# New order of the last attention pair's steps in a one-core decoder kernel, with its output halves, weight halves and row sums

## The reference

```python
for blk in range(S // Q_BLOCK):                       # Q_BLOCK = 128, 8 blocks
    s = einsum(q[:, :, q0:q1], k[:, :, :q1]) * scale  # 16 heads of 64
    s = s + c[:, :, q0:q1, None] - c[:, :, None, :q1] # forget gates, cumulated
    p = softmax(where(mask, s, -inf))
    outs.append(einsum(p, v[:, :, :q1]))
o = concatenate(outs)...reshape(B, S, D_MODEL)
h = h + o @ w_o
h = h + swiglu(rmsnorm(h, norm_ffn[layer]), w_ffn_in[layer], w_ffn_out[layer])
```

## Time and profile before

| | us |
|---|---|
| median of 3 runs | 2259.54 (2257.51 to 2260.15) |
| the profiled execution, its own time | 2259.69 |
| its span, first to last instruction | 2257.9 |
| TensorE busy | 2211.3 (98%) |
| DVE, ACT, POOL busy | 1684.8, 1182.4, 364.0 |
| mean granted TensorE clock | 0.997 |

### The profile page before, as it was taken

How to read it: one execution, slowest core, us unless ns; L and a number is a source line. 1 busy time by engine, 2 the same in 40 slices (tenths; PEclk the granted TensorE clock), 3 DMA queues, 4 the chain that set the end, 5 groups by cost and what they waited for, 6 DMA issues and landing times.

```text
span 2257.9 us, 28937 instructions
## 1 busy us (share of the span) xinstructions
PE 2211.3 (98%) x10409; PEld 1836.0 (81%) x10409; DVE 1684.8 (75%) x2345; ACT 1182.4 (52%) x1871; POOL 364.0 (16%) x353
## 2 busy tenths in 40 slices
PE   8999999999999999999999999989999999999998
PEld 6788877788888888878888888867888888888886
DVE  7667778777778887687766767664768888888866
ACT  5543466355555555256666666653525555555525
POOL 4000000022222222021111111102101222222210
PEclk9999999999999999999999999999999999999999
DMA  5120301366666666331111111122135666666662
GB/s 150 47 59 27 92 4 35 131 131 131 130 131 131 131 131 128 115 113 29 38 29 38 38 38 37 29 93 66 56 112 108 127 130 128 126 132 127 129 170 84
DMA packets 208828, 207.85 MB, mean 92 GB/s; under 512 B 9688, under 2 KB 153280, under 8 KB 208704
## 3 DMA queue, kind: packets, MB, share of 16 engines
q0 software_dynamic: 39168, 75.51, 20.3%
q1 hardware_dynamic: 167808, 126.43, 18.9%
q10 hardware_dynamic: 1728, 4.31, 0.8%
HBM read 122.28 MB, written 83.95 MB: 91 GB/s over the span
## 4 chain that ended last, share of the span: by engine, by line
PE 85%; DVE 8%; ACT 3%; issue 2%; DMA 1%; ACTq 1%; POOL 0%; DVEq 0%
PE ps L1207 36%; PE ps L1039 16%; PE ps L1295 14%; PE ps L1407 7%; PE ps L1452 3%; PE ps L1439 3%; PE ps L1539 2%; PE ps L1419 1%; PE ps L1420 1%; DVE rxl L2223 1%; ACT kh L2068 1%; DVE qs L2949 1%; DMA rinv_dram<-rinv_rows 0%; DVE resid L2243 0%; PE ps L1379 0%
## 5 line engine op out<-in xcount | busy, mean ns | idle before, releaser
L967 POOL DMA_DIRECT2D spill<-c x256 | 224.1, 928 | 727.6 <-DVE c L2613 498.4
L2482 DVE TENSOR_TENSOR ring_l<-raw_ffn,ring_h 128x512 fp32r<-128x512 f32 x320 | 223.1, 699 | 154.3 <-ACT ring_h L1766 152.9
L1766 ACT ACTIVATE ring_h<-raw_ffn 128x512 fp32r<-128x512 f32 x320 | 198.8, 625 | 198.8 <-PE ps L1207 103.9
L1859 ACT ACTIVATE c<-ps 128x512 f32<-128x512 f32 x256 | 150.2, 597 | 13.2
L2104 ACT ACTIVATE probs<-ps,nmax 128x896 f32<-128x896 f32 (+7 forms) x128 | 95.1, 743 | 103.5 <-DVE nmax L3018 101.7
L1407 PE MATMUL ps<-xh,wh_att 128*128 128x512 f32 x368 | 148.8, 404 | 0.0
L1766 ACT ACTIVATE ring_h<-w_sum 128x512 fp32r<-128x512 f32 x112 | 69.6, 625 | 146.6 <-PE ps L1039 38.9
L1407 PE MATMUL ps<-xl,wh_att 128*128 128x512 f32 x368 | 144.1, 392 | 0.0
L1407 PE MATMUL ps<-xh,wl_att 128*128 128x512 f32 x368 | 144.0, 391 | 0.0
L3025 DVE TENSOR_TENSOR ptl<-ps,pth 128x512 fp32r<-128x512 f32 (+1 forms) x160 | 97.1, 635 | 58.2 <-ACT pth L2139 57.1
L2613 DVE TENSOR_TENSOR c<-ps,c 128x512 f32<-128x512 f32 x192 | 123.6, 686 | 4.7 <-PE ps L1295 4.4
(11 more groups left out here) (400 smaller groups left out, 6352.4 us busy)
## 6 DMA issues: line engine op xcount, KB each, us to landing
spill<-c POOLq DMA_DIRECT2D x256, 256.0 KB, 5.9
raw_ffn<-in_w_ffn_in SPq DMA_DIRECT2D x88, 512.0 KB, 5.3
raw_ffn<-in_w_ffn_out SPq DMA_DIRECT2D x44, 512.0 KB, 7.5
resid<-spill SPq DMA_DIRECT2D x24, 512.0 KB, 7.3
raw<-in_w_rec_in SPq DMA_DIRECT2D x16, 512.0 KB, 5.5
spill<-resid POOLq DMA_DIRECT2D x16, 512.0 KB, 2.9
raw_att<-in_w_kvf SPq DMA_DIRECT2D x16, 512.0 KB, 4.0
xin<-in_x SPq DMA_DIRECT2D x4, 1024.0 KB, 9.9
```

The lines of the kernel that those rows point to most:

```text
L967: pool.dma_start(spill[m, :, half * BANK:(half + 1) * BANK], block[:, :], accum_op=ALU.add).then_inc(sem, 16)
L1766: act.activation(F.ring_h[slot][:, :], src, ACT.Copy).then_inc(F.unit_hi, 1)
L1859: act.activation(dst[:, :], y if what == "s5" else w, ACT.Copy).then_inc(out_tapped, 1)
L2482: dve.tensor_tensor(F.ring_l[slot][:, :], src, F.ring_h[slot][:, :].bitcast(F32), ALU.subtract).then_inc(F.unit_lo, 1)
```

## The change

It gives the last pair's units a new order of steps, with the same steps in each unit except for p, of which units now have 2, 5, 1, 6, 3, 4, 4 and 3 where they had 5, 2, 4, 3, 5, 2, 4 and 3. It moves the halves of the output and of the output weights to other steps. R comes ahead of the last unit's T0, and R's transpose waits for the second exponential of that unit too (in every pair). In the last pair ACT issues the row sums' store at V1. DVE adds output tile 0 ahead of the low half of weight 3. For the other pairs the list is unchanged.

```diff
 LAST_UNIT_STEPS = [
-    "T0 T1 X Y p p p T2 V0 V1 T3 S0 S1 p V2 p V3",
-    "O T0 S0 S1 p V0 p",
-    "O T0 T1 S0 p V0 T2 S1 p V1 p V2 p",
-    "O T0 T1 S0 S1 p V0 p V1 p",
-    "O T0 T1 p p V0 T2 p V1 T3 S0 p V2 S1 p V3",
-    "O T0 S0 S1 p V0 p",
-    "O T0 T1 S0 p V0 T2 S1 p V1 p V2 p",
-    "O T0 T1 R p V0 p V1 p",
+    "T0 T1 X Y S0 T2 p T3 V0 V1 p S1 V2 V3",
+    "O p T0 S0 S1 p V0 p p p",
+    "O T0 T1 p V0 T2 V1 S0 S1 V2",
+    "O p p T0 T1 S0 p S1 p V0 p V1 p",
+    "O T0 T1 S0 p T2 V0 T3 V1 p S1 V2 V3 p",
+    "O T0 S0 S1 p p V0 p p",
+    "O T0 T1 S0 p p T2 V0 S1 p p V1 V2",
+    "O p R T0 T1 p p V0 V1",
 ]
...
-HIGH_O_AT = {(-1, "S1"): (0, 1), (-1, "B"): (2,), (0, "Y"): (3,), (0, "T3"): (4,), (1, "V0"): (5,),
-             (2, "V0"): (6,), (3, "S1"): (7,)}
-LOW_O_AT = {(-1, "S1"): (0,), (-1, "B"): (1, 2), (0, "T2"): (3,), (0, "S1"): (4,), (2, "T0"): (5,),
-            (2, "V2"): (6,), (3, "V0"): (7,)}
+HIGH_O_AT = {(-1, "A"): (0, 1), (-1, "B"): (2, 3), (0, "V1"): (4,), (2, "V0"): (5,), (3, "T1"): (6,),
+             (4, "T3"): (7,)}
+LOW_O_AT = {(-1, "S1"): (0,), (-1, "B"): (1,), (0, "S0"): (2,), (0, "V3"): (3, 4), (2, "S1"): (5,),
+            (3, "V1"): (6,), (5, "O"): (7,)}
...
-    OUT_HI_AT = {(-1, "A"): 0, (0, "S1"): 1, (UNITS - 1, "T0"): 2}
-    OUT_LO_AT = {(-1, "S1"): 0, (2, "O"): 1, (UNITS - 1, "T1"): 2}
+    OUT_HI_AT = {(-1, "A"): 0, (0, "Y"): 1, (UNITS - 2, "T2"): 2}
+    OUT_LO_AT = {(-1, "S1"): 0, (1, "S1"): 1, (UNITS - 2, "V2"): 2}
...
                     elif step == "R":
                         acc = claim(rsum_tile(i))
+                        slot, n = s_tile(i, UNITS - 1, 1)
+                        pe.wait_ge(drained[slot], n)
...
-                    if (u, step) == (UNITS - 1, "R"):
+                    if (u, step) == (UNITS - 1, "R" if with_p else "V1"):
                         act.wait_ge(drained[rsum_tile(i)[0]], rsum_tile(i)[1])
...
             for k in range(KT):
+                if k == 0:
+                    dve.wait_ge(reloaded[k], 32)
+                    add_tile(tiles.use("attE", k), k, OUT_ATT + k + 1)
                 if k < KT - 2:
                     if k != 2:
                         split_lo(pieces.use("attE", k + (3 if k < 2 else 2)))
                 else:
                     for n in range(2):
                         first_low(F1, 2 * (k + 2 - KT) + n)
-                dve.wait_ge(reloaded[k], 32)
-                add_tile(tiles.use("attE", k), k, OUT_ATT + k + 1)
+                if k > 0:
+                    dve.wait_ge(reloaded[k], 32)
+                    add_tile(tiles.use("attE", k), k, OUT_ATT + k + 1)
```

## The result

The changed kernel takes 2247.69 us (median of 5 runs, 2247.3 to 2248.19) against 2259.54 (2257.51 to 2261.14): ratio 0.9947, 95% interval 0.9936 to 0.9958. That is 11.85 us less, where 11.0 were forecast (2248.5, range 2245.5 to 2253.5). The profiled execution has a span of 2245.9 us, 12.0 less than before.

What follows compares the result with a forecast made beforehand. TensorE was taken as the bound, losing 14.3 us in the last pair and its tail. Gains of 1.0 + 0.3 + 4.2 + 2.7 + 1.2 + 0.6 + 1.0 = 11.0 us gave 2259.54 - 11.0 = 2248.5 us, range 2245.5 to 2253.5.

Steps and rivals of the forecast that it cites:

- Output halves at the start: Start of the last pair: high halves 0 and 1 made earlier, X waits 0.2 instead of 1.2 us; 1.0 gained.
- Unit 0: Last pair's first unit: V0's wait is spread over T2, V0 and V2; 1.35 of 1.65 us stay, 0.3 gained.
- Units 1 and 2: Last pair: stops before T2.0, p7 and V2.2 go; 4.8 us of stops become 0.6, 4.2 gained.
- Units 3 to 6: Last pair: p steps ahead of each T0 cover the exponentials; 3.2 us of stops become 0.5, 2.7 gained.
- The reload of tile 0: SP's reload of resid, landing about when DVE's early sum 1 wants it: taken as covered, 1.0 us at worst.
- Unit 7 and R: Last unit: stops before V7.0 (0.5 us) and the first wo matmul (0.7) both go; 1.2 gained.
- The added wait in the other seven pairs: R's new wait for the second drain: taken as 0, bound 0.05 us a pair; skill estimate up to 0.8 over eight pairs.
- Tail: Row sums to output: the k = 7 matmuls' 1.2 us stop shrinks; 0.6 gained, 0.7 stays, DMAs 0.5 either way.
- First sum: First output tile's sum ahead of a weight half, so tile 3 no longer starts late: 1.0 us gained, 0.1 perhaps lost.
- The layout: Four queues laid out in order from trace durations: 14.8 us of stops for the old order, trusted to about half a microsecond.

Runs made afterwards that it cites:

- the steps alone: The kernel before with only the new order of steps, R's place and wait, and ACT's store at V1: 2256.19 us, ratio 0.9986.
- the further order: The changed kernel with another order of steps and other places of output and weight halves: 2246.18 us, 0.9939; run again, 2245.64 us.
- the first sum: The kernel before with only the sum of output tile 0 moved ahead of weight half 3: 2258.83 us, ratio 0.9995.
- the output halves alone: The kernel before with only the new places of the output halves: 2256.52 us, ratio 0.9986.
- the order with V behind T: The changed kernel with every V straight behind its T and all p steps at their unit's end: 2269.82 us, ratio 1.0041.

## Why the prediction was right

The sum was 14.3 us of stops less 3.3; in the trace after they are some 2.7 (the four waits and what the pipeline loses at each, and five hesitations under 0.3), and the pair length fell by 11.61. The other 0.24 of the 11.85 is of the size of the 0.31 by which the two profiled executions were apart ahead of the pair.

- *Output halves at the start:* 0.2 was to stay before X, 0.29 did. *Unit 0:* T2, V0 and V2 were to lose 0.7, 0.5 and 0.15, and lose 0.57, 0.42 and 0.23.
- *Units 1 and 2:* 0.2 before p7 and 0.4 before V2.0; measured 0.13 and 0.37. *Units 3 to 6:* 0.1 and 0.4; measured 0.09 and 0.20. The reload of tile 0 is not waited for.
- *Unit 7 and R:* both stops gone, R at 1511.50 (1511.6 forecast), reciprocal to 1512.79 (1512.9). But the parts of this line are not worth the same. With the old units, R and store (everything but the order of steps) the first output matmul does not wait either, and the stop at the first k = 7 matmul is 0.1 us. With R and the store moved and weight half 2 left, in the steps alone, the first output matmul still waits 0.5. So it is weight half 2, made in unit 6, that takes the stop before the first output matmul away, and the new units that take V7.0's (0.37 stays with the old ones); no run shows a gain from R's new place.
- *The added wait in the other seven pairs* was taken as 0: the R transposes of the last five of them are 61.53 to 61.60 us apart, and 61.56 to 61.64 before. From the first to the seventh it is 369.80 us, before 369.87. The Trainium skill's 50 to 100 ns for a sequencer's read of a semaphore ("Advanced Engine Details and Errata", section "Network/Comms") would, if it stood in line once a pair, have made that 0.3 to 0.6 us longer (an estimate), and it is not.
- *Tail, the mis-sized term:* 0.7 was to stay and 0.34 did. The step that was wrong is "the broadcast is issued behind ACT's last o_low (1515.26)": it is issued 0.06 us after o_low starts, at 1514.93, 0.33 earlier. The DMAs themselves took 4.78 us to POOL's start; 4.66 were assumed. In the second trace of the changed kernel they took 4.55, and the stop was 0.1. Over the fourteen traces they took 4.48 to 5.38, so part of how small this stop is belongs to the execution and not to the order.
- *First sum:* 1.0 gained and nothing lost; tile 3 starts as the last k = 7 matmul lets it (1528.37, then 1528.82, two matmuls of 0.23).
- *The layout against the others:* by its own totals of stops (14.8 us before, 3.0 in the changed kernel, 2.0 in the further order) its difference to the pair length of before was within 0.8 us wherever the clock stayed at 1.00 (the further order is the 0.8), and wrong by 1.1 and 6.3 where it fell. The misses of the runs with the first sum (0.3) and the output halves alone (0.4) are no larger than what the wait for the row sums grew: the broadcast took 4.97 and 5.38 us there, where the layout has 4.66.

What the prediction's parts don't say, and the runs do: a part's price hangs on the others. The output halves were given 1.0 for X and bits of other lines; alone they are worth 2.9, and taking them from the changed kernel costs 4.4. The steps alone are worth 3.3, and their loss costs 4.2. The places where a half is made were fitted to the new order, and each without the other brings a stop of its own: 1.6 us before p4 with the halves alone, 1.5 before T2 with the steps alone.

## What to carry to other kernels

When several in-order engines follow one written list, lay the queues out by the durations of the trace before changing the list, and check the layout on the old order first: here that gave 14.8 us of stops for an 80 us stretch where the trace has 14.3. Move list and side work together, since each alone brings new stops. Look for the independent matmuls (p steps) that stand where nothing waits, and put them between the transposes or scores and the step that waits for their results.

## What was not expected of the hardware

The granted TensorE clock can fall in the midst of a busy kernel. In the run with the steps alone no stop was over 1.89 us, and the two ahead of the fall were 1.02 and 1.54: 2.56 us idle of 3.8 were followed by 0.50 for 2 us and 0.65 for 2 more, at a matmul every 0.43 us instead of 0.23, and cost 1.2 us. In the order with V behind T it was 0.50 over 5 us and under 1.00 in seven windows of 5. The same two stops in the changed kernel with the old output halves left it at 1.00, so what decides it is not settled here. In their traces the kernels before and after stay at 1.00 in this stretch, so none of the 11.61 us is clock; but a forecast for a worse order has to allow for it.
